# Expert rows: a table of token sums with an adding indirect DMA, in place of a table of expert rows gathered at the end

## Chip, core and metric

The kernel runs on one core of a Trainium2 chip, in float32. The metric is the device time of one execution in microseconds (us), lower is better. The kernel before takes 2435.93 us (median of three runs, 2430.61 to 2442.70).

## What is computed

Two transformer blocks over 512 tokens of width 1024. The change lies in the last part of the second block, the routed experts: 32 experts, each token goes to its four best, and an expert's work is done in blocks of up to 64 rows (slots).

```python
top_vals, top_idx = lax.top_k(logits, TOP_K)              # TOP_K = 4
gates = softmax(top_vals)
# per expert e, on the rows routed to it:
gt = minimum(xb @ w_gate[e] + b_gate[e], 7); up = clip(xb @ w_up[e] + b_up[e], -7, 7)
hid = gt * sigmoid(1.702 * gt) * (up + 1.0)
y_rows = hid @ w_down[e] + b_down[e]
out = zeros.at[row_tok].add(y_rows * row_gate)            # sum of a token's four rows
x = layer_norm(2 ** 0.25 * h + out, ln2_g, ln2_b)
```

## The kernel before

The program is a sequence of stages, each with its own block of instructions per engine and a barrier after it. Everything before the experts (a state-space block, attention, a feed-forward block, the second block's token mixer and router) takes the first 1336 us. The change touches four places: `stage_ffn`, `stage_route`, `stage_experts`, and the shared buffers.

**Routing** (`stage_route`). A one-hot matmul builds, for each slot (column) and partition, the number of the token whose row is worked on there, and its gate. A slot holds 64 rows. Partition p < 64 stands for the first half (512 numbers) of row p, partition 64 + p for its second half, so `G.slot_tokens` holds `2 * token + half`: a row number of the DRAM table `h_halves` (1024 rows of 512). Beside it, `G.choice_row` holds for each token and each of its four choices the row of the table `expert_rows` where the result will lie. A slot's unused rows have gate 0.

**The expert loop** (`stage_experts`). One pass works on one slot. There are 45 passes here for 32 experts (experts with more than 64 rows take more than one). An expert's matrices are three of 4 MB (gate, up, down), loaded by SyncE's queue (SP) as four parts of 1 MB each, two neighbouring matrix rows to a partition, into `expert_ring`: one place for each of the three and a fourth for the next expert's gate matrix, which ScalarE (ACT) copies over (L2405). A part is loaded as soon as the last pass of the expert before has used it (`used`, `moved`), so each pass can also wait for its matrices (`landed`). The order of the experts (`LONG_FIRST`, `PERIOD`) mixes those with more slots among those with one.

TensorE (PE) goes through pass i in this order (L2486): gate product's first half; `turn_up(i-1)` (four transposes); `turn_x(i+1)` (four transposes of the rows of the next slot, which GpSimd has gathered into `slot_x`); gate product's second half; `down(i-1)`; `turn_gate(i)`; up product. Each product has 16 matmul calls (32 instructions). ACT copies products from PSUM; VectorE (DVE) adds biases, clamps, multiplies, and makes in `result(i-1)` (L2555) the tile `slot_y`, the down product times the gates.

GpSimd (POOL) has one task in the loop (L2323): after `turn_x(i)` it copies the row numbers of slot i+1 and issues the indirect DMA (gather) into `slot_x`:

```python
pool.wait_ge(q["x_turned"], i + 1)
gather(i + 1)
```

In pass i+1 ACT stores `slot_y` of slot i with two DMAs (L2394) to `expert_rows`; DVE waits for that (`y_out`) before it writes `slot_y` anew.

**The bias sums.** In the first two passes PE forms `gates @ b_down` for each of the four tiles of 128 tokens (`bias_sum`, L2455), and DVE adds it to `2 ** 0.25 * h` in `G.X` (`add_bias`, L2557).

**The tail.** After the last store has landed, POOL issues 16 indirect gathers from `expert_rows` (`choice`, L2341), three of them adding to what is in SBUF already, because their target is in use; DVE adds thirteen pieces to `G.X` and does the layer norm tile by tile (L2583 to L2602); SP stores the tiles. Rows of `expert_rows` that no pass writes are set to zero in `stage_ffn` (L1279).

Of the kernel before, what the change touches and what calls it, by code (L numbers as in the profile page):

```python
# [1207 lines left out]
def stage_ffn(nc, A, G):  # L1208


    with ExitStack() as ctx:
# [51 lines left out]
        @block.sync  # L1263
        def _(sp):
            ln.load(sp)
            G.W.upto(sp, G.W.index[("q2",)] + RING)
            sp.wait_ge(G.y_zeroed, 16 * (-(-(MAX_SLOTS - EXPERTS) * CAP // P)))
# [6 lines left out]
        def _(act):  # L1274

            act.wait_ge(zeros_ok, 1)
            for r in range(EXPERTS * CAP, MAX_SLOTS * CAP, P):
                n = min(P, MAX_SLOTS * CAP - r)
                act.dma_start(G.y_dram[r:r + n, :], zeros[0:n, :]).then_inc(G.y_zeroed, 16)  # L1279
# [688 lines left out]
def stage_route(nc, A, G):  # L1968
# [6 lines left out]
    with ExitStack() as ctx:  # L1975
# [20 lines left out]
        rowf = sb("choice_rowf", [P, TK])  # L1996
# [84 lines left out]
        def _(dve):  # L2081
# [61 lines left out]
            for h in range(2):  # L2143
# [10 lines left out]
            step(nc.vector.scalar_tensor_tensor(out=rowf[:], in0=sl[:], scalar=float(CAP), in1=col[:], op0=ALU.mult,  # L2154
                                                op1=ALU.add))
            nc.vector.tensor_copy(G.choice_row[:], rowf[:])
# [11 lines left out]
            nc.vector.tensor_scalar(G.slot_tokens[:], ps[:, 3, 0:LIST], upper[:, 0:1], None, ALU.add).then_inc(list_ok, 1)  # L2168

# [51 lines left out]
def stage_experts(nc, A, G):  # L2221
# [5 lines left out]
    with ExitStack() as ctx:  # L2227
# [21 lines left out]
        row_in = [sem(f"ex_row_in{c}") for c in range((T - 1) * TOP_K)]  # L2249
        sum_in, pair_in = sem("ex_sum_in"), sem("ex_pair_in")  # L2250
        pair = X.ring[:, 0, KB - 1, :]

        def plain(n):
            return X.ring[:, X.MATS, n, :] if n < KB else X.ring[:, 0, n - KB, :]
# [26 lines left out]
        def _(sp):  # L2281
# [26 lines left out]
        def _(pool):  # L2308
# [32 lines left out]
            def choice(dst, t, k, sem, add=False):  # L2341
                c = t * TOP_K + k
                at = bass.IndirectOffsetOnAxis(G.choice_row[:, c:c + 1], 0)
                if add:
                    nc.gpsimd.indirect_dma_start(dst, None, G.y_dram[:, :], at, compute_op=ALU.add).then_inc(sem, 16)  # L2345
                else:
                    nc.gpsimd.indirect_dma_start(dst, None, G.y_dram[:, :], at).then_inc(sem, 16)  # L2347
            def four(t):
                for k in range(TOP_K):
                    n = t * TOP_K + k  # L2350
                    choice(plain(n), t, k, row_in[n])
            end = T - 1
            four(0)
            choice(G.X[:, end, :], end, 0, sum_in, True)
            choice(pair, end, 2, pair_in)
            four(1)
            pool.wait_ge(sum_in, 16)
            choice(G.X[:, end, :], end, 1, sum_in, True)
            pool.wait_ge(pair_in, 16)
            choice(pair, end, 3, pair_in, True)  # L2360
            four(2)

        @block.scalar
        def _(act):
# [370 lines left out]
```

## Time and profile before

| | |
|---|---|
| median of three runs | 2435.93 us (2430.61 to 2442.70) |
| profiled execution, its own time | 2436.61 us |
| its span in the trace | 2434.8 us (1.8 us lie around it) |
| first transposes of `slot_x` in the expert stage | at 1336.6 us |
| last matmul ends, DVE starts the last `slot_y` | 2383.3 us |
| end of the span | 2434.8 us |
| busy over the span | PE 2275.0 us (93%), DVE 807.1, ACT 652.7, POOL 206.5 |
| mean granted TensorE clock | 0.959 |
| DMA, whole span | 570.75 MB, 234 GB/s; in the expert loop up to 423 GB/s |

How to read it: times are microseconds from the start of the span. The profile names an instruction by engine, line and operation, `out<-in`. PEclk is the share of the full TensorE clock that was granted (1.00 is 2.4 GHz, 0.50 is 1.2 GHz). "DMA share" is the busy share of the 16 DMA engines. In a timeline the bracket gives the idle time of the engine before the instruction and what ended it. For a DMA issued by POOL, "to landing" runs from the start of POOL's instruction, which first writes the descriptors, to the last byte.

### The profile page before, as it was taken

What the parts mean: (1) busy time and instruction counts of PE and PEld (TensorE: products, weight loads), DVE (VectorE), ACT (ScalarE), POOL (GpSimd) and SP (SyncE); (2) the same over time, 40 slices, a digit from 0 to 9 for tenths busy, and PEclk for the clock granted to TensorE, in tenths of its full rate; (3) what the DMA queues carried; (4) which work ended last, traced back from release to release, by engine and by line L of the source; (5) the groups of instructions that cost most, each with busy time, mean ns of one, the idle gap of its engine ahead of it and who ended that gap; (6) DMA issues with size and microseconds to landing.
All of it is one profiled execution on the core that took longest, in us unless ns stands there. A gap on an engine that the chain in (4) does not pass through costs nothing. (4 is left out here: it accounts for less than half of the span.)

```text
span 2434.8 us, 27490 instructions
## 1 busy us (share of the span) xinstructions
PE 2275.0 (93%) x9835; PEld 1094.8 (45%) x9836; DVE 807.1 (33%) x1548; ACT 652.7 (27%) x854; POOL 206.5 (8%) x239
## 2 busy tenths in 40 slices
PE   6998999989899999989896999999999999999991
PEld 4444656634557567544445333333333333333330
DVE  1411556644444454532434212112111112112125
ACT  1211222221000000001301444444344444444440
POOL 1003111100000000000300000000000000000003
PEclk8999999989999999999896999999999999999995
DMA  8344233210621311141006869999999999999995
GB/s 332 130 191 113 78 87 104 80 68 0 257 102 71 137 69 70 52 157 38 0 27 256 340 240 390 420 423 408 423 422 411 422 408 419 423 406 423 421 381 177
DMA packets 139863, 570.75 MB, mean 234 GB/s; under 512 B 12280, under 2 KB 47277, under 8 KB 88589
## 3 DMA queue, kind: packets, MB, share of 16 engines
q1 hardware_dynamic: 123584, 527.89, 54.8%
q0 software_dynamic: 6432, 21.66, 2.5%
q10 hardware_dynamic: 9772, 20.25, 2.2%
q8 instruction: 42, 0.69, 0.1%
q14 instruction: 33, 0.26, 0.0%
HBM read 545.57 MB, written 24.18 MB: 234 GB/s over the span
## 5 line engine op out<-in xcount | busy, mean ns | idle before, releaser
L2405 ACT COPY expert_ring<-expert_ring 128x2048 f32 x180 | 331.7, 1896 | 70.8 <-DMA expert_ring<-in_w_gate_dram 59.0
L2472 PE MATMUL banks<-expert_ring,slot_xT_gate 128*64 128x512 f32 x1440 | 328.4, 598 | 1.5 <-issue 0.8
L2472 PE MATMUL banks<-expert_ring,hiddenT 128*64 128x512 f32 x1440 | 319.6, 597 | 2.1 <-DVE hiddenT L2547 2.1
L2472 PE MATMUL banks<-expert_ring,slot_xT_up 128*64 128x512 f32 x1440 | 319.6, 595 | 0.8 <-DMA expert_ring<-in_w_up_dram 0.6
L2472 PEld LDWEIGHTS banks<-expert_ring,hiddenT 128*64 128x64 f32 x1440 | 104.0, 138 | 209.5 <-issue 207.2
L2472 PEld LDWEIGHTS banks<-expert_ring,slot_xT_gate 128*64 128x64 f32 x1440 | 100.1, 137 | 188.6 <-issue 181.4
L2472 PEld LDWEIGHTS banks<-expert_ring,slot_xT_up 128*64 128x64 f32 x1440 | 99.1, 137 | 187.1 <-issue 175.9
L2555 DVE TENSOR_SCALAR slot_y<-banks,slot_gates 128x512 f32<-128x512 f32 x45 | 33.8, 750 | 412.4 <-PE banks L2472 412.4
L486 PE MATMUL banks<-hT,weight_ring 128*128 128x512 f32 x320 | 142.6, 605 | 2.3 <-PEq L2642 2.3
L2540 DVE TENSOR_TENSOR up_act_T<-banks,expert_bias_T 128x512 f32<-128x512 f32 x45 | 31.1, 691 | 310.0 <-PE banks L2434 310.0
L1355 PE MATMUL banks<-hT,weight_ring 128*128 128x256 f32 x512 | 114.4, 383 | 4.3 <-PEq L2642 3.3
L1071 PE MATMUL banks<-weight_ring,mix_scaled 128*128 128x512 f32 x256 | 113.6, 605 | 3.5 <-DVE mix_scaled L1109 3.5
L723 PE MATMUL banks<-hT,weight_ring 128*128 128x512 f32 x256 | 115.1, 603 | 0.0
L2379 ACT COPY gate_product<-banks 128x512 f32<-128x512 f32 x45 | 26.4, 586 | 318.3 <-PE banks L2472 318.3
L1355 PEld LDWEIGHTS banks<-hT,weight_ring 128*128 128x128 f32 x512 | 98.1, 192 | 20.5 <-issue 7.0
L486 PEld LDWEIGHTS banks<-hT,weight_ring 128*128 128x128 f32 x320 | 61.4, 194 | 80.8 <-issue 80.8
L1349 PE MATMUL banks<-weight_ring,hidden_T 128*128 128x512 f32 x192 | 84.1, 593 | 0.9 <-PE banks L1355 0.9
L2317 POOL COPY slot_ids<-slot_tokens 128x1 int32 (+1 forms) x45 | 8.2, 183 | 897.6 <-PE banks L2434 897.6
L1355 PE MATMUL banks<-token_half_sums,weight_ring 128*128 128x256 f32 x384 | 84.2, 379 | 0.0
L1071 PEld LDWEIGHTS banks<-weight_ring,mix_scaled 128*128 128x128 f32 x256 | 49.4, 194 | 64.8 <-issue 59.2
L1355 PEld LDWEIGHTS banks<-token_half_sums,weight_ring 128*128 128x128 f32 x384 | 73.0, 190 | 9.9
L723 PEld LDWEIGHTS banks<-hT,weight_ring 128*128 128x128 f32 x256 | 48.1, 193 | 56.2 <-issue 56.2
(440 smaller groups left out, 2500.9 us busy)
## 6 DMA issues: line engine op xcount, KB each, us to landing
expert_ring<-in_w_gate_dram SPq DMA_DIRECT2D x128, 1024.0 KB, 13.5
expert_ring<-in_w_up_dram SPq DMA_DIRECT2D x128, 1024.0 KB, 12.8
expert_ring<-in_w_down_dram SPq DMA_DIRECT2D x128, 1024.0 KB, 10.9
weight_ring<-in_w_ada_dram SPq DMA_DIRECT2D x12, 2048.0 KB, 11.1
weight_ring<-in_w_in_dram SPq DMA_DIRECT2D x8, 2048.0 KB, 14.7
weight_ring<-in_w_ff_in_dram SPq DMA_DIRECT2D x8, 2048.0 KB, 11.1
weight_ring<-in_w_ff_out_dram SPq DMA_DIRECT2D x8, 2048.0 KB, 13.3
weight_ring<-in_w_in_dram SPq DMA_DIRECT2D x24, 512.0 KB, 6.6
```

The lines of the kernel that those rows point to most:

```text
L486: m = nc.tensor.matmul(ps[:, n % 4, :], w[:, k, b * P:(b + 1) * P], G.hT[:, k, :], start=(k == 0), stop=(k == KB - 1))
L723: x = nc.tensor.matmul(out, w[:, k, :], G.hT[:, k, :], start=(k == 0), stop=(k == KB - 1))
L1071: m = nc.tensor.matmul(ps[:, banks[h], :], mix[:, k, t * P:(t + 1) * P], w[:, k % 4, h * HALF:(h + 1) * HALF], start=(k == k0), stop=(k == ...
L1349: m = nc.tensor.matmul(out, x[:, k, j * P:(j + 1) * P], y[:, k, :], start=(k == 0), stop=(k == 3))
L1355: m = nc.tensor.matmul(out[:, b, :], y[:, k, at:at + P], x[:, k, :], start=(k == 0), stop=(k == 3))
L2317: nc.gpsimd.tensor_copy(ids[:], G.slot_tokens[:, at]).then_inc(q["ids_ok"], 1)
L2379: nc.scalar.copy(gate_tok[:], ps[:, B_G, :]).then_inc(q["g_copied"], 1)
L2405: nc.scalar.copy(flat_ring[:, c * size:(c + 1) * size], flat_ring[:, bass.ds(source + c * size, size)])\
L2472: x = nc.tensor.matmul(ps[h * CAP:(h + 1) * CAP, bank, :], lhs[:, k % 4, (k // 4) * CAP:(k // 4 + 1) * CAP], X.ring[:, m, k, h * HALF:(h + ...
L2540: nc.vector.tensor_tensor(up[:], turned_product(B_UT), cols, ALU.add).then_inc(q["u_biased"], 1)
L2555: nc.vector.tensor_scalar(y[:], ps[:, B_D, :], G.slot_gates[:, at], None, ALU.mult).then_inc(q["y_ok"], 1)
```

## The change

Rows are no longer stored to `expert_rows` and gathered at the end. A table `token_sums` in DRAM (2048 rows of 512: 1024 for the tokens' halves, 1024 spare) is first filled with `2 ** 0.25 * h + gates @ b_down`, and each pass adds its `slot_y` to it with one indirect DMA that adds (`add_rows`). At the end the table is read back with four plain loads.

- `stage_ffn`: four DMAs of zeros (the spare rows) in place of sixteen (the unused rows of `expert_rows`).
- `stage_route`: `choice_row` (two instructions) goes; five small DVE instructions after `slot_tokens` form `slot_rows`: for a used row its number `2 * token + half`, for an unused one a spare row.
- POOL: in pass i, `add_rows(i-1)` follows `gather(i+1)`; it waits for `slot_y`, and in pass 1 also for the table (`table_in`). After the loop `add_rows(last)` takes the place of the 16 gathers.
- ACT: `store` goes; in the first two passes four plain DMAs of 512 KB write `G.X` to the table (`to_table`), tile by tile.
- PE and DVE: `bias_sum(2)`, `bias_sum(3)` and their `add_bias` move to an earlier place in pass 1.
- Tail: SP loads the four tiles from the table; DVE has no additions left, only the layer norm.

```diff
 @block.gpsimd
+            def add_rows(i):
+                at = slice(i, i + 1) if isinstance(i, int) else bass.ds(i, 1)
+                pool.wait_ge(q["y_ok"], i + 1)
+                nc.gpsimd.tensor_copy(rows[:], G.slot_rows[:, at]).then_inc(rows_ok, 1)
+                pool.wait_ge(rows_ok, i + 1)
+                if not (isinstance(i, int) and i == 0):
+                    pool.wait_ge(held_rows, i)
+                nc.gpsimd.tensor_tensor(row_tick[:], tick[:, 0:1], tick[:, 0:1], ALU.add).then_inc(held_rows, 1)
+                nc.gpsimd.indirect_dma_start(G.sum_dram[:, :], bass.IndirectOffsetOnAxis(rows[:, 0:1], 0), y[:], None,
+                                             compute_op=ALU.add).then_inc(G.y_out, 16)
             def body(i, first):
                 pool.wait_ge(q["x_turned"], i + 1)
                 gather(i + 1)
+                if first:
+                    pool.wait_ge(table_in, 16 * T)
+                add_rows(i - 1)
...
-            pool.wait_ge(G.y_out, last * 32 + 32)
+            add_rows(last)
+            pool.wait_ge(G.y_out, last * 16 + 16)
             nc.gpsimd.tensor_tensor(tick[:, 2:3], tick[:, 0:1], tick[:, 0:1], ALU.add).then_inc(q["stored"], 1)
-            pool.wait_ge(q["bias_added"], T)
...
 @block.scalar
-            def store(i):
-                act.wait_ge(q["y_ok"], i + 1)
-                for h in range(2):
-                    act.dma_start(G.y_dram[bass.ds(i * CAP, CAP), h * HALF:(h + 1) * HALF],
-                                  y[h * CAP:(h + 1) * CAP, :]).then_inc(G.y_out, 16)
+            def to_table(t):
+                act.wait_ge(q["bias_added"], t + 1)
+                act.dma_start(table(t), G.X[:, t, :]).then_inc(table_in, 16)
...
                 move_gate(i + 1)
-                if not (isinstance(i, int) and i == 0):
-                    store(i - 1)
                 sigmoid(i)
+                if first:
+                    to_table(2 * i)
                 up_copy(i)
+                if first:
+                    to_table(2 * i + 1)
                 x_for_up(i + 1)
 @block.sync
+            sp.wait_ge(q["stored"], 1)
+            for t in range(T):
+                sp.dma_start(G.X[:, t, :], table(t)).then_inc(sums_in[t], 16)
 @block.vector
             def body(i, first):
                 hidden(i - 1)
+                if first:
+                    add_bias(2)
+                    add_bias(3)
                 result(i - 1, first)
                 dve.wait_ge(q["hT_ok"], i)
-                if first:
-                    add_bias(2)
                 gate(i)
-                if first:
-                    add_bias(3)
...
             for t in range(T):
                 x = G.X[:, t, :]
-                for k in range(TOP_K if t < T - 1 else 0):
-                    dve.wait_ge(row_in[t * TOP_K + k], 16)
-                    step(nc.vector.tensor_tensor(x, x, plain(t * TOP_K + k), ALU.add))
-                if t == T - 1:
-                    dve.wait_ge(sum_in, 32)
-                    dve.wait_ge(pair_in, 32)
-                    step(nc.vector.tensor_tensor(x, x, pair, ALU.add))
+                dve.wait_ge(sums_in[t], 16)
                 nc.vector.bn_stats(stats[:, t, 0, :], x[:, 0:HALF])
```

Not shown are the removed function `choice` with its 16 calls (L2341 to L2361) and the small instructions of `stage_route`.

On POOL, the loop of the passes from the second on, before (`slot_ids` are the row numbers of the gather, `tick` is a one-element instruction between):

```order
L2271 UNCONDITIONAL_BRANCH
L2271 ISA
L2317 ISA
L2317 COPY slot_ids<-slot_tokens 128x1
L2318 REGISTER_ALU
L2312 TENSOR_TENSOR tick<-tick 1x1
L2320 DMA slot_x<-h_halves,slot_ids 128x512
L2271 ISA
L2271 COMPARE_AND_BRANCH
```

and with the change (`slot_rows_now` are the row numbers of the adding DMA):

```order
L2276 ISA
L2325 ISA
L2325 COPY slot_ids<-slot_tokens 128x1
L2326 REGISTER_ALU
L2320 TENSOR_TENSOR tick<-tick 1x1
L2328 DMA slot_x<-h_halves,slot_ids 128x512
L2335 ISA
L2335 COPY slot_rows_now<-slot_rows 128x1
L2339 TENSOR_TENSOR row_tick<-tick 1x1
L2340 DMA token_sums<-slot_y,slot_rows_now 2048x512
L2276 ISA
L2276 COMPARE_AND_BRANCH
```

Behind each gather now stands the adding DMA of two slots earlier, and the next pass's gather stands behind that one on the same engine.

On ACT with the change, the end of pass 0, from the sigmoid of pass 0 on:

```order
L2390 ACTIVATE gate_sigmoid_T<-gate_act_T 128x512
L2394 DMA token_sums<-X 128x1024
L2386 COPY up_product<-banks 128x512
L2394 DMA token_sums<-X 128x1024
L2374 COPY slot_xT_up<-banks 128x512
```

The same five rows stand once more at the end of pass 1: the fourth tile's write to the table is issued behind the copy of pass 1's up product.

## Rows read from the trace of the kernel before

**Rows 1.** busy time by stretch: PE, PEld, DVE, ACT, POOL (us), PEclk, DMA share, GB/s

```profile
1400.00:1500.00 100.00, 100.00 (x476) 36.42 (x474) 20.05 (x32) 46.59 (x41) 8.07 (x12) 1.00 0.77 304
1570.00:2300.00 730.00, 728.39 (x3456) 265.78 (x3454) 140.60 (x225) 326.06 (x290) 64.57 (x96) 1.00 1.01 418
```

**Rows 2.** chain that ended last, three stretches of the loop: start us, us, what

```profile
1889.62 20.90 DMA expert_ring<-in_w_up_dram
...
2209.88 20.90 DMA expert_ring<-in_w_up_dram
...
2282.08 1.16 PE banks L2434 x8
...
2293.69 0.68 PE banks L2434 x4
...
2304.82 1.16 PE banks L2434 x8
```

**Rows 3.** who waited for whom, 1500 to 2300, engine PEld: us, times, longest

```profile
PEld banks L2472 <- DMA expert_ring<-in_w_up_dram: 5.5, 8, 1.5
```

**Rows 4.** DMA queues in one pass, 2239.4 to 2262.1: packets, MB, share

```profile
q1 hardware_dynamic: 1239, 9.06, 95.6%
q10 hardware_dynamic: 160, 0.26, 3.0%
```

**Rows 5.** timeline of one pass: start us, us, engine, line, operation [idle <-releaser]

```profile
2283.41 0.18 POOL L2317 COPY slot_ids<-slot_tokens 128x1 int32 x1 [20.48 <-PE banks L2434]
...
2284.26 1.40 POOL L2320 DMA_INDIRECT slot_x<-h_halves,slot_ids  x1 [0.15 <-issue]
...
2286.65 7.04 PE L2472 MATMUL banks<-expert_ring,hiddenT 128*64 128x512 f32 x32
...
2293.93 0.75 DVE L2555 TENSOR_SCALAR slot_y<-banks,slot_gates 128x512 f32<-128x512 f32 x1 [9.14 <-PE banks L2472]
```

**Rows 6.** tile slot_x: the gathers on POOL, and their time to landing

```profile
L2320 POOL DMA_INDIRECT slot_x<-h_halves,slot_ids x45: 987/1397/1400, 1338.5 to 2329.7; - x45
...
DMA to landing us min/median/max: 3.4/7.3/7.7
```

**Rows 7.** timeline, POOL: the second gather, with no DVE work beside it

```profile
1346.80 0.18 POOL L2317 COPY slot_ids<-slot_tokens 128x1 int32<-128x1 int32 x1 [7.26 <-PE banks L2434]
...
1347.55 0.99 POOL L2320 DMA_INDIRECT slot_x<-h_halves,slot_ids  x1 [0.30 <-issue]
```

**Rows 8.** line L2345, the three gathers that add: time on POOL, time to landing

```profile
L2345 POOL DMA_INDIRECT X<-expert_rows,choice_row x2: 1722/1921/2120, 2392.9 to 2403.3; - x2
L2345 POOL DMA_INDIRECT expert_ring<-expert_rows,choice_row x1: 2569/2569/2569, 2405.3 to 2405.3; - x1
...
DMA to landing us min/median/max: 8.4/8.6/9.3
```

**Rows 9.** DMA queue q0, 2402 to 2403.5 (plain), then 2410 to 2411.5 (adding)

```profile
q0 software_dynamic: 165, 0.59, 101.8%
...
q0 software_dynamic: 88, 0.30, 104.3%
```

**Rows 10.** timeline of the last down product and of the tail

```profile
2373.11 9.96 PE L2472 MATMUL banks<-expert_ring,hiddenT 128*64 128x512 f32 x32 [2.09 <-DVE hiddenT L2547]
...
2383.31 0.75 DVE L2555 TENSOR_SCALAR slot_y<-banks,slot_gates 128x512 f32<-128x512 f32 x1 [10.26 <-PE banks L2472]
...
2427.48 0.69 DVE L2592 BATCH_NORM_STATS2 ln2b_stats<-X 128x6 f32<-128x512 f32 x1
...
2430.50 1.28 DVE L2601 SCALAR_TENSOR_TENSOR X<-X,ln2b_mv,hT 128x1024 f32<-128x1024 f32 x1
```

**Rows 11.** tile out_dram, four stores of 512 KB: time to landing

```profile
DMA to landing us min/median/max: 2.6/4.2/6.1
```

**Rows 12.** timeline, pass 1: ACT's copy of the up product

```profile
1386.68 0.59 ACT L2385 COPY up_product<-banks 128x512 f32<-128x512 f32 x1 [4.69 <-PE banks L2472]
```

**Rows 13.** stretch of the last down product (columns as in rows 1)

```profile
2373.10:2379.00 5.90, 5.89 (x14) 1.71 (x16) 0.00 (x0) 0.00 (x0) 0.00 (x0) 0.51 0.02 8
```

More of the change, by code:

```diff
@@ L1266, in _ @@
             G.W.upto(sp, G.W.index[("q2",)] + RING)
-            sp.wait_ge(G.y_zeroed, 16 * (-(-(MAX_SLOTS - EXPERTS) * CAP // P)))
+            sp.wait_ge(G.spare_zeroed, 16 * T)
         @block.gpsimd
@@ L1276, in _ @@
             act.wait_ge(zeros_ok, 1)
-            for r in range(EXPERTS * CAP, MAX_SLOTS * CAP, P):
-                n = min(P, MAX_SLOTS * CAP - r)
-                act.dma_start(G.y_dram[r:r + n, :], zeros[0:n, :]).then_inc(G.y_zeroed, 16)
+            for t in range(T, 2 * T):
+                rows = G.sum_dram[2 * t * P:2 * (t + 1) * P, :].rearrange("(p h) n -> p (h n)", h=2)
+                act.dma_start(rows, zeros[:]).then_inc(G.spare_zeroed, 16)
             for g in range(FG):
@@ L1995, in stage_route @@
         col = sb("choice_col", [P, TK])
-        rowf = sb("choice_rowf", [P, TK])
+        token_row = sb("slot_token_row", [P, LIST])
+        spare = sb("slot_spare", [P, LIST])
+        empty = sb("slot_empty", [P, LIST])
         colhot = sb("col_onehot", [P, TK, P])
@@ L2168, in _ @@
             nc.vector.tensor_scalar(G.slot_tokens[:], ps[:, 3, 0:LIST], upper[:, 0:1], None, ALU.add).then_inc(list_ok, 1)
+            nc.vector.tensor_scalar(token_row[:], ps[:, 3, 0:LIST], upper[:, 0:1], None, ALU.add)
+            step(nc.vector.tensor_scalar(empty[:], ps[:, 3, LIST:2 * LIST], 0.0, None, ALU.is_equal))
+            step(nc.vector.tensor_scalar(spare[:], token_row[:], -1.0, tok[:, 0:1], ALU.mult, ALU.add))
+            step(nc.vector.scalar_tensor_tensor(out=spare[:], in0=spare[:], scalar=2.0 * S, in1=empty[:], op0=ALU.add,
+                                                op1=ALU.mult))
+            nc.vector.tensor_tensor(G.slot_rows[:], token_row[:], spare[:], ALU.add)
 def paired_rows(src, j):
@@ L2248, in stage_experts, with table @@
         held = sem("ex_held")
[L2249 to L2254, printed above, removed]
+        rows, row_tick = sb("slot_rows_now", [P, 1], I32), sb("row_tick", [1, 1])
+        rows_ok, held_rows, table_in = sem("ex_rows_ok"), sem("ex_held_rows"), sem("ex_table_in")
+        sums_in = [sem(f"ex_sums_in{t}") for t in range(T)]
+        def table(t):
+            return G.sum_dram[2 * t * P:2 * (t + 1) * P, :].rearrange("(p h) n -> p (h n)", h=2)
         stats = sb("ln2b_stats", [P, T, 2, 6])
@@ L2334, in _ @@
             pool.wait_ge(G.xg_in, last * 16 + 32)
-            pool.wait_ge(G.y_out, last * 32 + 32)
+            add_rows(last)
+            pool.wait_ge(G.y_out, last * 16 + 16)
             nc.gpsimd.tensor_tensor(tick[:, 2:3], tick[:, 0:1], tick[:, 0:1], ALU.add).then_inc(q["stored"], 1)
             pool.wait_ge(q["stored"], 1)
-            pool.wait_ge(q["bias_added"], T)
[L2341 to L2361, printed above, removed]
         @block.scalar
@@ L2423, in _ @@
             last = loop(act, body)
-            store(last)
             nc.scalar.activation(tick[:, 3:4], tick[:, 0:1], ACT.Sqrt).then_inc(q["root_ok"], 1)
@@ L2496, in body @@
                 turn_x(i + 1)
+                if first and not zero:
+                    bias_sum(2)
                 product(xTg, B_G, 0, range(PARTS // 2, PARTS), now, None if zero else i)
+                if first:
+                    bias_sum(0 if zero else 3)
                 if not zero:
                     down(i - 1, before, not first)
-                if first:
-                    bias_sum(0 if zero else 2)
                 turn_gate(i)
@@ L2506, in body @@
                 product(xTu, B_U, 1, range(PARTS), now)
-                if first:
-                    bias_sum(1 if zero else 3)
+                if zero:
+                    bias_sum(1)
             X.turn_bias(pe, ps, 1).then_inc(q["bias_turned"], 1)
@@ L2564, in body @@
                 hidden(i - 1)
+                if first:
+                    add_bias(2)
+                    add_bias(3)
                 result(i - 1, first)
                 dve.wait_ge(q["hT_ok"], i)
-                if first:
-                    add_bias(2)
                 gate(i)
-                if first:
-                    add_bias(3)
             dve.wait_ge(G.h_out, 16 * T)
```

11 lines of the change are left out of this document (4 added, 7 removed).

## The prediction, made before the changed kernel ran

> **What bounds the kernel now.** I read the busy time by stretch first, then the chain that ended last, then the DMA queues, and last the timeline of one pass. In the loop from 1570 to 2300 us TensorE is busy 728.39 of 730.00 us at the full clock, and the 16 DMA engines have a share of 1.01 at 418 GB/s; only from 1400 to 1500 do they have room (0.77) [rows 1]. So two resources are full at once. The chain shows a pass as TensorE's own work: from 2282.08 to 2304.82 us, that is 22.74 us [rows 2]. It also shows that every seven passes a part of an up matrix lands just when it is needed: such waits begin at 1889.62 and at 2209.88 us, 320.26 us apart for 14 passes, or 22.88 us a pass [rows 2], and the weight loads waited eight times for up parts, 5.5 us in all [rows 3]. Nothing is left over on the DMA engines there: in one pass the expert matrices take a share of 95.6% and the stores of `slot_y` 3.0% [rows 4].
>
> About 0.5% (12 us) is what a measurement of this kernel can tell from no change. The sum below is made against the profiled execution's own 2436.6 us, 0.7 us above the median of the runs.
>
> **The tail: 20 us less.** Before, from the start of the last `slot_y` at 2383.31 us [rows 10] to the end of the span are 51.5 us. With the change: `slot_y` is done at 2384.06. POOL wakes 0.17 us after its releaser (the transposes end at 2283.24 [rows 2], the copy starts at 2283.41), and needs 0.85 us from that copy to its DMA instruction [rows 5]: 2385.1. The adding DMA on a quiet core: the fastest gather lands 3.4 us after its start [rows 6]; I add 0.8 us for descriptors and 0.7 us for the transfer (both below), so it lands at about 2390.0. The tick on POOL and SP's issue take 0.4 us, a load of 512 KB 4.2 us (the stores of that size have this median [rows 11]), so DVE starts at 2394.6. A tile of the layer norm takes 4.3 us (2427.48 to 2430.50 + 1.28 [rows 10]), four take 17.2: 2411.8. The last store took 3.0 us to the end of the span: 2414.8, which is **20.0 us** earlier. Bounds: 15 (the adding DMA lands after 9.3 us [rows 8]) and 22 (the load lands after 2.6 us [rows 11]).
>
> **The first table: 16.5 us more.** `add_rows(0)` in pass 1 waits for all four writes of `G.X` to the table, and the fourth is issued by ACT behind `up_copy(1)`, so after pass 1's up product. Behind that wait stands, on POOL, the gather for slot 3, which TensorE needs at `turn_x(3)` in pass 2. Count from the end of the up product: the copy is done after 0.64 us (0.59 and a wake of 0.05 [rows 12]), the write is issued at 0.75, lands after 6 us (my choice between 4.2 and something above 6.1 [rows 11], since weights are loading) at 6.75. Then POOL: 0.17 + 0.85 + 2.0 (descriptors of the adding DMA) + 0.3 + 0.75 + 6.9 (gather, both from the next part) = 10.97, so the rows are there at 17.7. TensorE is there 3.9 us after the up product (11.61 less 0.68 less 7.04, below). It stands still for 13.8 us. After an idle stretch of 2.09 us before the last down product the granted clock was 0.51 [rows 13], the lower level of 1.2 GHz, and the product took 9.96 us [rows 10] in place of 7.04 [rows 5]: 2.9 us more. Together 16.7, say **16.5 us**. Bounds: 7 (table in 4.2 us, descriptors 1.0, gather 3.4, no fall of the clock) and 21.
>
> **The loop: 30 us more.** Two things are added to each pass, and both end in TensorE's waits.
>
> First the order on POOL. Until now the gather for slot i+2 started right behind `turn_x(i+1)`. Now it stands behind `add_rows(i-1)`, which waits for `slot_y` of `down(i-1)` in the same pass. Count from the end of that product, at 2293.69 us [rows 2]. `slot_y` is done at 2294.68, so at 0.99 [rows 5]. POOL wakes (0.17) and reaches its DMA instruction (0.85) at 2.01. Writing descriptors takes a plain gather 1.40 us in the loop [rows 6] and 0.99 without DVE work beside it [rows 7], an adding one 1.72 to 2.57 us in the tail [rows 8]: I take 2.0, since DVE works beside only part of it, and get 4.0. Then 0.3 us between two such instructions, 0.75 us from copy to DMA instruction with DVE quiet [rows 7]: 5.06. A gather lands 7.3 us after its start [rows 6], less the 0.4 us by which its descriptors are now faster: 11.96. TensorE needs the rows at `turn_x`: the eight transposes of the next pass end at 2305.98 and the last four take 0.68 [rows 2], so at 2305.30, or 11.61. It waits **0.4 us** a pass. The unshown price is that of the adding DMA in front: low end 1.0 us of descriptors, the rows are 0.6 us early; high end 2.57 us and a gather that lands as late as the slowest adding one, 9.3 us [rows 8], a wait of 3.4 us. I take the inner value because adding DMA and gather are issued 3 us apart, more than the DMA engines need for either.
>
> Second the DMA engines. An adding DMA keeps them longer for the same bytes: 165 plain packets of 0.59 MB in 1.5 us against 88 adding ones of 0.30 MB [rows 9], so 2.6 against 5.2 us for a MB. The store took 3.0% of a pass, 0.68 us [rows 4]; the adding DMA of the same 0.26 MB takes 1.36, **0.7 us** more a pass. Where the engines are full, from 1570 us to the end of the loads at some 2370, that is 35 passes: 24 us. Before that there is room.
>
> The two waits overlap: an idle stretch for one lets the other catch up. I count the 24 us, and 6 us for the passes before 1570 us and for passes in which the gather is the later one. Low end nothing, if loads and gathers find room; high end 3.4 us in each of 42 passes, 143 us, and then the clock: if it falls behind each of them as it did behind the idle 2.09 us, 2.9 us more a pass, 122 us.
>
> **At nothing.** TensorE's work is the same; bias sums only change places, each `add_bias` (1.2 us) has a half gate product of 3.6 us beside it. ACT loses two DMA issues a pass and waits for TensorE anyway. The zeros in `stage_ffn` are written beside matmuls that show no gap; five short DVE instructions in `stage_route` run while POOL prepares the first gather. If that cover were gone they cost about 1 us.
>
> **Sum:** 2436.6 - 20 + 16.5 + 30 = **2463 us**.
>
> **A page against the row.** The gather's 7.3 us carry the loop's first term [rows 6]. The Trainium skill, "DMA: Bandwidth & Descriptors", section "Anatomy of one DMA", fits a DMA issued from GpSimd as 2.0 us plus its bytes at 436 GB/s, which is an estimate of 2.6 us for these 256 KB. The trace does not agree: the row is 4.7 us above the page's figure, with the DMA engines at a share of 1.01, and the row decides.
>
> **The rivals.**
> - **Gathers land as on a quiet core** (3.4 us, least of [rows 6], in place of 7.3). Then they are never late in the loop, only the 24 us of the DMA engines remain, and the start is 3.5 us shorter: 2436.6 - 20 + 13 + 24 = 2454 us. Against it: the median is near the maximum of 7.7. The page's fit named above would have it come out this way.
> - **The loop becomes a chain through POOL.** It decides where the gather's wait is well above the 0.7 us a pass of the DMA engines; if the clock falls behind the waits too, slower products lie on the same chain. With 1.85 us (2.57 us of descriptors, 0.85 and 7.7 us for the gather) it is 2436.6 - 20 + 16.5 + 78 = 2511 us, with 3.4 us and the clock up to 2698. For it: descriptors in the tail took up to 2.57 us. Against it: less loading while TensorE waits should make gathers faster.
> - **The loop takes it for nothing.** The additional 0.7 us fit in and gathers come in time; the start costs its 16.5 us or somewhat less: about 2436 us, no difference. For it: SP waits for free buffers in most passes.
> - **Faster, by the tail.** As the last, and the wait for the first table costs only its lower bound of 7 us: 2436.6 - 22 + 7 = 2422 us. It decides at a start and a loop that cost less than 8 us together. For it: from 1400 to 1500 us the DMA engines had room. Against it: the fourth write lies behind an up product, whatever the transfer takes.
>
> **How the numbers follow.** My forecast has a chance of 0.45 (2450 to 2490 us), the chain through POOL 0.20, quiet gathers 0.07, nothing in the loop 0.15, faster by the tail 0.13. Slower by over 0.5% are the first three: 0.72. Within 0.5%: 0.15. Faster: 0.13. The range of 2430 to 2550 leaves out the last rival and the upper part of the chain through POOL, 2 in 10 together.
>
> **What would show it.** TensorE waiting at L2434 for `slot_x` in most passes, or for up parts longer than before, with passes of 23.2 to 23.7 us between the same transposes; one wait of 10 to 17 us near 1393 us, with PEclk at 0.50 behind it; the adding DMA at twice the store's share; 31 us from the last `slot_y` to the end. I am wrong if passes stay at 22.8 us (then the loads had room), if they exceed 25 us (then the chain through POOL rules), or if the wait near 1393 us is missing.

## The result, and the profile after

The changed kernel takes **2559.12 us** (median of 4 runs, 2557.15 to 2563.89) against 2435.55 us: the ratio is 1.0514, 95% interval 1.0494 to 1.0534, so it is 5% slower. The forecast was 2463 us with a range of 2430 to 2550. The span of the profiled execution is 2562.2 us, 127 us more than before.

The stretches of [rows 1], in the trace after. Columns: stretch, us, then PE, PEld, DVE, ACT, POOL busy, PEclk, DMA share, GB/s.

```profile
1400.00:1500.00 100.00, 92.34 (x418) 33.17 (x420) 15.68 (x25) 40.13 (x36) 14.49 (x24) 0.94 0.64 233
1570.00:2300.00 730.00, 673.18 (x3022) 240.84 (x3020) 122.17 (x196) 282.15 (x252) 101.49 (x168) 0.96 0.94 365
```

Neither of the two resources that were full is full any more: TensorE is busy 673 of 730 us, the DMA engines have a share of 0.94, and the granted clock is below 1. Something else sets the pace. The waits of TensorE name it (engine, line, waited for; us, times, longest), from 1300 us on:

```profile
PE banks L2434 <- DMA slot_x<-h_halves,slot_ids: 98.8, 43, 12.5
```

and the gathers themselves, in the tile view of `slot_x`, which answers to [rows 6]:

```profile
L2328 POOL DMA_INDIRECT slot_x<-h_halves,slot_ids x45: 987/1028/1049, 1336.7 to 2488.9; - x45
...
DMA to landing us min/median/max: 3.5/9.3/10.0
```

No wait for an up matrix [rows 3] is left. TensorE waits for the gather in 41 of the 42 passes behind the 12.5 us at the start (the last of the 43 waits lies at the start too), and the gather's median landing went from 7.3 to 9.3 us although its descriptors are written faster (1.03 in place of 1.40 us). One pass on POOL and on TensorE, in the timeline (start, us, engine, line, operation, idle before and its releaser), answers to [rows 5]:

```profile
1796.04 7.04 PE L2472 MATMUL banks<-expert_ring,hiddenT 128*64 128x512 f32 x32
...
1804.25 0.18 POOL L2335 COPY slot_rows_now<-slot_rows 128x1 int32 x1 [20.30 <-DVE slot_y L2557]
...
1805.04 1.84 POOL L2340 DMA_INDIRECT token_sums<-slot_y,slot_rows_now  x1 [0.34 <-issue]
...
1807.50 1.03 POOL L2328 DMA_INDIRECT slot_x<-h_halves,slot_ids  x1 [0.15 <-issue]
...
1816.86 0.90 PE L2434 MATMUL banks<-ident,slot_x 128*128 128x128 f32 x4 [1.98 <-DMA slot_x<-h_halves,slot_ids]
1817.69 5.13 PE L2472 MATMUL banks<-expert_ring,slot_xT_gate 128*64 128x512 f32 x16
```

The down product ends at 1803.08, the gather starts 4.42 us later and lands 9.3 us after that; TensorE stands idle 1.98 us. Then the second half of the gate product takes 5.13 us; before, it took 3.65 us in every one of these passes. The stretch of that half (columns as above) has a granted clock of 0.69, a mixture of the two levels of 2.4 and 1.2 GHz:

```profile
1817.70:1822.60 4.90, 4.90 (x17) 1.56 (x18) 0.00 (x0) 0.00 (x0) 0.00 (x0) 0.69 1.01 428
```

The page's group for the whole gate products puts a sum on that, before and after:

```profile
L2472 PE MATMUL banks<-expert_ring,slot_xT_gate 128*64 128x512 f32 x1440 | 328.4, 598 | 1.5 <-issue 0.8
```

```profile
L2472 PE MATMUL banks<-expert_ring,slot_xT_gate 128*64 128x512 f32 x1440 | 373.2, 666 | 0.7 <-ACT slot_xT_gate L2371 0.7
```

The same 1440 matmuls take 44.8 us more. Counted over the timeline, 27 of the 42 second gate halves of the loop were slow (4.8 to 5.4 us each), the other 15 took 3.65 us. The waits ahead of the slow ones were 1.72 to 2.62 us long, those ahead of the others up to 2.31, so the length of the wait alone doesn't decide it. The passes are of two lengths, 24.5 to 25.4 and 26.2 to 27.3 us, mean 26.08 against 22.81.

The start and the tail, again from the timeline:

```profile
1394.33 0.18 POOL L2335 COPY slot_rows_now<-slot_rows 128x1 int32<-128x1 int32 x1 [47.90 <-DMA token_sums<-X]
...
1403.15 1.12 PE L2434 MATMUL banks<-ident,slot_x 128*128 128x128 f32 x4 [12.47 <-DMA slot_x<-h_halves,slot_ids]
1404.21 5.36 PE L2472 MATMUL banks<-expert_ring,slot_xT_gate 128*64 128x512 f32 x16
...
2531.51 0.75 DVE L2557 TENSOR_SCALAR slot_y<-banks,slot_gates 128x512 f32<-128x512 f32 x1 [9.08 <-PE banks L2472]
...
2533.20 1.59 POOL L2340 DMA_INDIRECT token_sums<-slot_y,slot_rows_now  x1 [0.33 <-issue]
2538.25 0.18 POOL L2361 TENSOR_TENSOR tick<-tick 1x1 f32<-1x1 f32 x1 [3.46 <-DMA token_sums<-slot_y,slot_rows_now]
```

**Where the time is:** the tail is 30.7 us long (2531.51 to 2562.2) in place of 51.5, so -20.8. The waits for `slot_x` are 98.8 us: 12.5 at the start, 84.1 in the 41 waits of the loop (2.05 each), and 2.2 for one of the first gathers, which was waited for before as well (2.5), so +96.3. The gate products are +44.8, the transposes of `slot_x`, slower behind a wait, +6.4 (36.5 in place of 30.1). Together +126.7 of the +127.4 us; terms of under 4 us, which go both ways, are left out.

### The profile page after: what moved, and what is told of

It reads as the page before. It is cut to its first block and busy times, and to the rows that moved or that the text cites. A ratio compares the mean times of both kernels' runs of the same rounds, so it can differ in the third digit from the quotient of the medians.

```text
span 2562.2 us, 27405 instructions
## 1 busy us (share of the span) xinstructions
PE 2329.9 (91%) x9835; PEld 1107.3 (43%) x9836; DVE 793.3 (31%) x1538; ACT 652.3 (25%) x854; POOL 258.1 (10%) x358
## 5 line engine op out<-in xcount | busy, mean ns | idle before, releaser
L2472 PE MATMUL banks<-expert_ring,slot_xT_gate 128*64 128x512 f32 x1440 | 373.2, 666 | 0.7 <-ACT slot_xT_gate L2371 0.7
L2472 PEld LDWEIGHTS banks<-expert_ring,slot_xT_gate 128*64 128x64 f32 x1440 | 110.2, 152 | 223.6 <-issue 217.2
L2434 PE MATMUL banks<-ident,slot_x 128*128 128x128 f32 x184 | 36.5, 325 | 98.8 <-DMA slot_x<-h_halves,slot_ids 98.8
L2335 POOL COPY slot_rows_now<-slot_rows 128x1 int32 (+1 forms) x45 | 8.2, 182 | 999.4 <-DVE slot_y L2557 951.5
L1355 PEld LDWEIGHTS banks<-hT,weight_ring 128*128 128x128 f32 x512 | 98.1, 192 | 20.5 <-issue 7.0
L486 PEld LDWEIGHTS banks<-hT,weight_ring 128*128 128x128 f32 x320 | 61.0, 193 | 80.1 <-issue 80.1
L1349 PE MATMUL banks<-weight_ring,hidden_T 128*128 128x512 f32 x192 | 84.1, 593 | 0.9 <-PE banks L1355 0.9
L2340 POOL DMA_INDIRECT token_sums<-slot_y,slot_rows_now x45 | 82.5, 1833 | 15.3 <-issue 15.3
```

Of the source, the lines that this page charges most:

```text
L486: m = nc.tensor.matmul(ps[:, n % 4, :], w[:, k, b * P:(b + 1) * P], G.hT[:, k, :], start=(k == 0), stop=(k == KB - 1))
L1349: m = nc.tensor.matmul(out, x[:, k, j * P:(j + 1) * P], y[:, k, :], start=(k == 0), stop=(k == 3))
L1355: m = nc.tensor.matmul(out[:, b, :], y[:, k, at:at + P], x[:, k, :], start=(k == 0), stop=(k == 3))
L2340: nc.gpsimd.indirect_dma_start(G.sum_dram[:, :], bass.IndirectOffsetOnAxis(rows[:, 0:1], 0), y[:], None, compute_op=ALU.add).then_inc(G.y_ ...
L2434: m = nc.tensor.transpose(ps[:, bank, j * P:(j + 1) * P], paired_rows(src, j), G.ident[:])
L2472: x = nc.tensor.matmul(ps[h * CAP:(h + 1) * CAP, bank, :], lhs[:, k % 4, (k // 4) * CAP:(k // 4 + 1) * CAP], X.ring[:, m, k, h * HALF:(h + ...
```

## The experiments

The expectations name the experiments by label: e1 add later, e2 plain scatter, e3 gather first, e4 the fourth write to the table earlier, e5 and e9 plain scatter with a pause, e6 later and plain, e7 and e8 `move_gate` split, e10 adding with a pause, e11 another order of loads. The ratios are against the kernel before on the same chip: 2433.39 us for e1 to e4 (19 runs), 2433.58 for e5 to e8 (9), 2434.24 for e9 to e11 (15). A difference under 0.5% is taken as none.

### The order on POOL

**Add later.** POOL adds the rows of slot i-2 behind gather(i+1), so that no wait for `slot_y` of the same pass stands ahead of a gather. The diff leaves out two lines on the counting of `row_tick`.

```diff
             def body(i, first):
                 pool.wait_ge(q["x_turned"], i + 1)
                 gather(i + 1)
-                if first:
+                if not first:
                     pool.wait_ge(table_in, 16 * T)
-                add_rows(i - 1)
+                    add_rows(i - 2)
...
+            add_rows(last - 1)
             add_rows(last)
```

> Edit: pass i adds slot i-2's rows (ready half a pass after the gather of slot i+1 was issued) in place of slot i-1's, so GpSimd is free again when the next gather is due. Theory A (order on POOL: the gather starts 4.4 us after the down product and queues behind the adding DMA): TensorE waits for slot_x in no pass, the wait near 1390 us goes too, granted clock 1.00 through the loop. Theory B (the doubled engine time of the adding DMA slows the loads and all that hangs on them): waits for up parts stay or grow, the time stays above 2500. By A alone 2435.5 - 21 = 2415 us; with the predicted 24 us of DMA engine time on top, 2439 us.

Measured: 2429.23 us, ratio 0.9983 (0.9973 to 0.9993): no difference from before. The 124 us are gone with one step of POOL's order, with every add intact, so theory B falls; the time lies between the two values given for A. In its trace the gathers land at 7.3 us again, with the same adding DMAs on the same queue, each now issued 11.4 us ahead of the next gather in place of 2.5. What is left shows in the waits of TensorE from 1570 to 2300 us:

```profile
PE banks L2435 <- ACT up_product L2387: 12.1, 5, 3.8
```

**Gather first.** The other way round: POOL still waits for `slot_y`, but then issues gather(i+2) ahead of the adding DMA (gather(2) goes ahead of the loop; the diff leaves out that line and a longer `slot_tokens`).

```diff
             def body(i, first):
-                pool.wait_ge(q["x_turned"], i + 1)
-                gather(i + 1)
                 if first:
                     pool.wait_ge(table_in, 16 * T)
+                pool.wait_ge(q["y_ok"], i)
+                pool.wait_ge(q["x_turned"], i + 2)
+                gather(i + 2)
                 add_rows(i - 1)
```

> Edit: POOL still waits for slot_y of slot i-1, but then issues the gather (of slot i+2) first and the adding DMA behind it. This takes away only the DMA in front of the gather. Theory A with the queueing as the larger part: the gather starts 1.9 us after the down product and lands after about 7.0 us, at 8.9 of the 11.6 us that there are, so no waits in the loop; a wait of some 9 us for the first table remains. 2435.5 - 21 + 12 = 2427 us, with 24 us of DMA engine time 2451 us. If the wait comes from the engines' load and not from the queue, the gather still takes over 9 us, and there are waits of about 0 to 1 us: 2440 to 2480 us.

Measured: 2446.16 us, ratio 1.0055 (1.0038 to 1.0072). From its tile view of `slot_x`:

```profile
DMA to landing us min/median/max: 3.3/7.2/8.4
```

Both experiments bring back 7.2 to 7.3 us. The time of gather first lies between the 2427 and the 2451 us of its expectation, nearer to the one with the adds' engine time. The two differ in the first wait: 11.0 us stay here, since POOL still waits for the table there.

**Plain scatter.** The order of the changed kernel, with `compute_op` taken off, so that the same bytes are written and not added (the sums are left out).

> Edit: the changed kernel with its per-pass DMA writing without adding (the sums are left out, so the layer norm works on other numbers). Theory A: the gather still starts 4.4 us after the down product, so it still waits; behind a DMA of half the engine time it should land some 0.7 us sooner than 9.3, so waits of about 1.3 us a pass in place of 2.1, fewer falls of the clock, 2490 to 2530 us. Theory B: with the adding gone the loop returns to 22.8 us a pass: about 2430 us.

Measured: 2429.54 us, ratio 0.9980 (0.9970 to 0.9991). The number is the one of theory B: the waits of 1.3 us a pass that A expected are missing. The gather starts 4.17 us after the down product and 2.21 us after the scatter, much as in the changed kernel, but in the loop it is in time (three waits of up to 0.3 us). Timeline of POOL, then the tile view of `slot_x`:

```profile
1810.70 1.24 POOL L2340 DMA_INDIRECT token_sums<-slot_y,slot_rows_now  x1 [0.33 <-issue]
...
1812.91 1.00 POOL L2328 DMA_INDIRECT slot_x<-h_halves,slot_ids  x1 [0.15 <-issue]
```

```profile
DMA to landing us min/median/max: 3.4/7.3/7.9
```

So the 2 us of landing are not the order alone and not the add alone: they need an adding transfer directly in front. The landings of the transfers in front show how the 2 us come about (medians in the loop). The plain scatter lands 7.3 us after its start and the gather 2.1 us behind it; in the changed kernel the adding DMA lands 9.8 us after its start and the gather 2.0 us behind it. Both transfers are still under way when the gather starts, but the adding one lands 2.5 us later, and the gather with it.

**Adding with a pause.** Is the gather's landing tied to its own start, or to the transfer in front? The changed kernel, adds intact, with an addition on POOL between the two that is there for its time alone:

```diff
+        pause_cols = sb("pause_cols", [P, 500])
...
                 pool.wait_ge(q["x_turned"], i + 1)
+                pool.wait_ge(paused, i)
+                nc.gpsimd.tensor_tensor(pause_cols[:], pause_cols[:], pause_cols[:], ALU.add).then_inc(paused, 1)
                 gather(i + 1)
```

> The changed kernel (adds intact) with one POOL instruction over 128x500 floats, about 1.0 us, between the adding DMA and the gather. The gather starts 1.0 to 1.5 us later than in the changed kernel (5.4 to 5.9 us after the down product's end in place of 4.4). Theory 'the gather's packets stand behind the adding ones in the same queue, so that its landing is set by when those are through': slot_x lands at the same time as in the changed kernel, 8 to 8.3 us after the start in place of 9.3, and the time stays within 2552 to 2570. Rival 'each gather takes 9.3 us whenever it starts while an adding one runs': 1.0 to 1.5 us more per pass, 2595 to 2620.

Measured: 2563.55 us, ratio 1.0530 (1.0514 to 1.0546); the changed kernel has 1.0514. The gather starts 5.87 us after the down product (4.42 in the changed kernel), and in the pass shown TensorE begins on the rows 13.74 us after it (13.78). Timeline, then tile view:

```profile
1810.14 1.03 POOL L2330 DMA_INDIRECT slot_x<-h_halves,slot_ids  x1 [0.16 <-issue]
```

```profile
DMA to landing us min/median/max: 3.4/8.0/8.6
```

A start 1.45 us later costs nothing (passes of 26.11 in place of 26.08 us), and the gather again lands 2.0 us behind the adding transfer: that one sets the landing. The rival would have cost 1.0 to 1.5 us a pass.

### Lateness without an adding transfer

The plain scatter again (sums left out), with the pause between scatter and gather, once of 900 and once of 1500 columns.

> The kernel of e2_plain_scatter (the scatter doesn't add, so the sums are left out) with one more POOL instruction in each pass, an addition over 128x900 floats between the scatter and the gather's id copy, some 2.0 us by the 128x512 that took 1.04 and the 128x1024 that took 2.35. The gather then starts about 6.4 us after the down product's end, lands 7.3 us later, and is 2 us late in each pass, with no adding transfer anywhere. Theory 'the lateness is the whole loss, by itself and by the clock that falls after it': 2545 to 2560 us, waits of about 2 us for slot_x in all passes of the loop and gate halves of 5.1 to 5.4 us behind more than half of them. Rival 'the adding transfers are what costs, in engine time and in lateness both': the time stays within 2430 to 2500.

> The kernel of e5_plain_pause (scatter without adding, so the sums are left out) with the POOL instruction between scatter and gather widened from 128x900 to 128x1500 floats: 1.70 us there, so 2.8 us here. In e5 the gather started 6.0 us after the down product's end, slot_x came 1.1 to 1.2 us late in each pass, the clock stayed at 1.00 and the time was 2487. Here it starts about 7.1 us after and is late by 2.2 to 2.4 us, as in the changed kernel. Theory 'a wait of 2 us before the second gate half lets the clock fall, one of 1.1 us doesn't': gate halves of 5.1 to 5.4 us come back behind more than half of the waits, granted clock of the loop 0.95 to 0.97, 2545 to 2565 us. Rival 'the clock falls in the changed kernel for another reason, the adding transfers among them': only the longer wait, 1.1 us times 43 more, 2530 to 2538, and the clock stays at 1.00.

Measured: 2487.47 us, ratio 1.0230 (1.0206 to 1.0254), for the shorter; **2582.91 us**, ratio 1.0602 (1.0586 to 1.0618), for the longer. For each, the waits of TensorE and the stretch from 1570 to 2300; first 900 columns:

```profile
PE banks L2438 <- DMA slot_x<-h_halves,slot_ids: 60.1, 43, 11.5
```

```profile
1570.00:2300.00 730.00, 696.47 (x3258) 253.61 (x3258) 175.92 (x213) 303.16 (x270) 150.66 (x210) 1.00 0.97 394
```

then 1500 columns, with the page's group of the gate products as well:

```profile
PE banks L2438 <- DMA slot_x<-h_halves,slot_ids: 110.6, 43, 11.9
```

```profile
1570.00:2300.00 730.00, 666.95 (x2962) 237.62 (x2960) 187.40 (x193) 280.00 (x248) 167.63 (x193) 0.95 0.89 356
```

```profile
L2476 PE MATMUL banks<-expert_ring,slot_xT_gate 128*64 128x512 f32 x1440 | 385.5, 685 | 0.7 <-ACT slot_xT_gate L2375 0.7
```

The first expectation was set for a lateness of 2 us and got 1.17 (47.8 us in the 41 waits of the loop), since the gather started 5.9 and not 6.4 us after the down product and landed after 7.0: the time lies in the rival's range, but by a shorter lateness than either theory spoke of, so this run decided nothing, and the second was made for that. It shows what the lateness costs nearly alone: 3 of 42 gate halves were slow, and passes have a mean of 24.31 us, 1.5 over before. The second has 2.36 us (96.7 in 41 waits), 34 of 42 gate halves slow, 57 us more of gate products than before, passes of 26.67 us. It is slower than the changed kernel and contains no adding transfer. The pause also made VectorE's work longer (187 us busy in place of 122), but from 1570 to 2300 us TensorE waited for `slot_x` alone. So a late gather alone costs that much, by the wait and the clock behind it; and since TensorE waits for no matrix in the changed kernel, nothing there points to another cost of the adding DMA than that it makes the gather late. The time is 18 us above the range expected: 34 slow halves are more than the "more than half" that it was worked out with.

### The DMA engines

**Later and plain.** The first experiment without `compute_op` (sums left out).

> The kernel of e1_add_later with compute_op taken from the scatter (the sums are left out): what is left between e1's 2429 us and this is the adding itself. Theory 'the adding transfer's second 0.7 us of engine time per pass makes the gate matrices late, and that is what e1 lost': the passes of 23.6 to 26.9 us shrink to under 23.5, the wait of the up product's turns for its copy (12.8 us, 6 times in e1) goes, and the time is 2412 to 2420. Rival 'any indirect transfer of 256 KB there delays them': passes and time as in e1, 2426 to 2432.

Measured: 2411.38 us, ratio 0.9907 (0.9892 to 0.9923); against "add later" the adding costs 0.76%, or 18 us. That is the first theory's time, less 1 us, and TensorE's waits for the up copy are 2.4 us in place of 12.8. DMA queues, 1600 to 2290 us (packets, MB, share of 16 engines), adding and then plain:

```profile
q0 software_dynamic: 6576, 15.47, 8.8%
```

```profile
q0 software_dynamic: 4880, 15.99, 5.8%
```

3.0% of 690 us over some 30 passes are 0.69 us a pass, beside the 0.7 of the forecast. The mean pass goes from 23.19 to 22.85 us (14 us over 42 passes), and 2 us are in the tail. The long passes come every seventh pass, and the timeline of ACT and TensorE in the kernel that adds later shows how a late matrix reaches TensorE there:

```profile
1888.42 1.90 ACT L2405 COPY expert_ring<-expert_ring 128x2048 f32 x1 [9.06 <-DMA expert_ring<-in_w_gate_dram]
...
1899.37 0.57 ACT L2387 COPY up_product<-banks 128x512 f32<-128x512 f32 x1
...
1899.99 1.13 PE L2435 MATMUL banks<-ident,up_product 128*128 128x128 f32 x4 [3.76 <-ACT up_product L2387]
```

A gate matrix lands late, ACT waits 9.06 us for it with `up_copy` behind it in its own order, and TensorE waits 3.76 us for that copy.

**Two attempts to go round it.** Splitting `move_gate` on ACT, two parts ahead of the up copy and two behind, in "add later" and, alone, in the kernel before (there with one more wait on POOL after the loop, not shown):

```diff
                 x_for_gate(i + 1)
-                move_gate(i + 1)
+                move_gate(i + 1, range(PARTS // 2))
                 sigmoid(i)
...
                 up_copy(i)
...
                 x_for_up(i + 1)
+                move_gate(i + 1, range(PARTS // 2, PARTS))
```

> The kernel of e1_add_later (adds intact), and on ACT the copies of the next gate matrix are issued in halves: two parts before the sigmoid and the up product's copy, two behind them. In e1 the up product's copy stood behind four gate copies that waited up to 9.1 us for their matrix, and PE's turn of the up product waited for that copy 12.8 us in 6 waits, with the gate half behind it at the low clock. Theory 'the order on ACT turns the late gate matrix into a wait of PE': those waits go, 2410 to 2418 us. Rival 'the matrix itself is late': the wait moves to the second gate half, on the ring copies, and the time stays 2426 to 2432.

> The kernel before with the same reordering of the gate copies on ACT alone. It waits 3.2 us for the up copy in all (weight loads, four times), so by the theory of e7 it gains 2 to 5 us: 2428 to 2432. Rival 'the order on ACT is worth 15 us anywhere': 2420 or less. If the second gate half waits for its copies in steady passes: 2440 and more.

Measured: 2483.07 us (ratio 1.0203, 1.0189 to 1.0217) and 2499.77 us (1.0261, 1.0245 to 1.0277). In the first run both theories fall, in the second the two on the order on ACT; of its third case ("2440 and more") only the number came, since the waits for the copies are 4.1 us in all and those for up matrices 26.2. The waits for the up copy go, but TensorE now waits for matrices (first kernel, 1570 to 2300 us):

```profile
PE banks L2474 <- DMA expert_ring<-in_w_up_dram: 21.2, 37, 1.6
PE banks L2474 <- ACT expert_ring L2405: 14.2, 15, 1.5
PE banks L2474 <- DMA expert_ring<-in_w_down_dram: 6.5, 10, 0.9
```

with a DMA share of 0.97 there, where "add later" has 1.02. What fits: the later copies give the gate buffer back later, SP issues all loads in one order behind that wait, and the DMA engines run dry. SP's waits that an ACT copy ended did grow in that stretch, from 198.3 to 257.2 us; that they are the cause was not tried.

The other attempt moves a gate load on SP ahead of an up load, in "add later": `GATE_TURN = (0, 0, 2, 0, 2)` for `(0, 1, 2, 0, 2)`.

> The kernel of e1_add_later (adds intact) with SP's table of load orders changed at one place, GATE_TURN = (0, 0, 2, 0, 2) in place of (0, 1, 2, 0, 2): the gate matrix that landed late every seventh pass (9.1 us of wait on ACT, up to 3.8 us on PE behind it) is issued ahead of the up matrix and not behind it. Theory 'the DMA engines are full, so that whichever matrix gives way comes late': the wait moves to the up matrix, 2428 to 2440. Rival 'only the order is wrong': the long passes go, 2411 to 2420, which would be 1% under the kernel before.

Measured: 2431.92 us, ratio 0.9990 (0.9981 to 0.9999). The time is that of "add later" or slightly more, and the wait moved to the up matrix, as the first theory has it:

```profile
PE banks L2473 <- DMA expert_ring<-in_w_up_dram: 15.7, 17, 1.6
```

### The first table

The fourth write to the table is issued by ACT ahead of the up copy of pass 1, not behind it:

```diff
+                if first and not (isinstance(i, int) and i == 0):
+                    to_table(3)
                 up_copy(i)
-                if first:
-                    to_table(2 * i + 1)
+                if first and isinstance(i, int) and i == 0:
+                    to_table(1)
```

> Edit: the fourth write to the table is issued by ACT before its copy of pass 1's up product. Both theories: the write starts at about 1381.3 in place of 1386.6 us and lands at about 1390 in place of 1394.2, so the one wait of 12.5 us near 1390 becomes about 8 us; the loop stays as it is: 4 us less than the changed kernel, 2555 us.

Measured: 2553.62 us (2 runs), ratio 1.0494 (1.0473 to 1.0515), an interval that overlaps the changed kernel's. The time is near the 2555 us expected, but the wait of 8 us is not there; the first wait is nearly what it was:

```profile
1390.27 1.65 POOL L2340 DMA_INDIRECT token_sums<-slot_y,slot_rows_now  x1 [0.17 <-issue]
...
1399.93 1.12 PE L2436 MATMUL banks<-ident,slot_x 128*128 128x128 f32 x4 [12.17 <-DMA slot_x<-h_halves,slot_ids]
```

All of TensorE's work came 3 us earlier in this execution (the turn of the up product at 1387.01 in place of 1389.94), and the adding DMA 4.7 us earlier, so against TensorE it began some 1.7 us sooner: the fourth write, issued right behind the third, took 11.0 us to land in place of 7.6. And the gather behind the adding DMA took 7.4 us from its start to TensorE's turn (1392.54 to 1399.93), where it took 5.9 in the changed kernel (1397.21 to 1403.15), and that gave 1.5 us back. Whether the loads that were under way by then are the reason was not tried.

## Why the prediction was wrong

**The tail** held: -20.8 us against -20.0. Each piece came within 0.7 us of its cost; the quiet adding DMA took 5.05 us from its start to POOL's tick (2533.20 to 2538.25), for which the sum had 4.9.

**The first table** held in its size, in part because errors cancelled: a wait of 12.5 us against 13.8, at 1403 us with the slow gate half behind it. The fourth write landed after 7.6 us, not 6; POOL needed 1.0 us less from there to the gather, and the gather 1.0 us less to land. What the clock cost was 1.7 us (5.36 - 3.65) and not 2.9, since only half a product ran slowly. Together 14.2 us against 16.5. The experiment that adds later takes the wait for the table and the one for `slot_y` from in front of this gather, and its pass there takes 26.70 us in place of 39.34 (26.71 before). Gather first, which keeps the wait for the table, keeps 11.0 of the 12.5 us.

**The loop** is where it failed: +137 us (42 passes of 3.27 us) against +30. The right rival was "the loop becomes a chain through POOL", which had a chance of 0.20; its low case of 2511 us was still 48 us short, since it had no slower clock in it. By the forecast's own sign (passes over 25 us) that rival is the one. The step that failed is the term for the order on POOL, which put the wait at 0.4 us, with the words "I take the inner value because adding DMA and gather are issued 3 us apart, more than the DMA engines need for either". Term by term:

- **The start of the gather** was right, even cautious: 5.06 us forecast, 4.42 measured (the adding DMA took 1.84 us on POOL, and the gather's id copy overlapped it).
- **The landing** was mis-sized: 6.9 us forecast, 9.3 measured. The argument was about how long DMA engines work on one transfer (1.36 us), not about how long the transfer is under way: the adding one lands 9.8 us after its start in the loop, and the gather 2.0 us behind it. With a plain scatter in front, which lands after 7.3 us, the same gather lands at 7.3; with a pause ahead of it its landing stays where it was in the pass. The high end had the same 9.3 us, taken from the slowest adding gather of the tail [rows 8]; that is another kind of transfer in another place, so the agreement is chance. 4.42 + 9.3 less the 11.61 of the forecast is 2.1 us, and 2.05 was measured.
- **The clock** was left at the high end only. The forecast had seen it fall behind an idle stretch of 2.09 us [rows 10, 13] and costed it at 2.9 us for the last down product. At waits of 2.05 us in mean it fell behind 27 of 41, 43 us by the slow halves, 1.6 us each: only half a product ran slowly, not a whole one as in the 2.9. At 1.17 us it fell behind 3 of 41, at 2.36 behind 34. A wait's price here is not proportional to its length.
- **The DMA engines.** The engine time was sized right (0.69 us a pass), but in the changed kernel it shows in no wait for a matrix: while TensorE waits for gathers, the engines have a share of 0.94. Only where the gather is in time does it appear: 18 us for the whole kernel, 14 of them in the loop, where the forecast had 24. And it enters mostly not at an up matrix as forecast, but at a gate matrix, by way of ACT's order. "The two waits overlap" was therefore right in kind, and the wrong one of the two was counted.
- **The argument against the rival** ("less loading while TensorE waits should make gathers faster") fell: with a plain scatter and a DMA share of 0.89 gathers took 7.2 us (the pause of 1500 columns), at 1.01 they took 7.3.

The rival of gathers that land as on a quiet core found no support: in no run whose trace shows the landings did the gathers of the loop have a median under 7.0 us. The fit in the Trainium skill, "DMA: Bandwidth & Descriptors", section "Anatomy of one DMA", from which the estimate of 2.6 us for these bytes came, doesn't agree with these rows.

The Trainium skill, "DMA: Bandwidth & Descriptors", section "Two DMAs through the same engine are not ordered", says that within one queue of a DMA engine descriptors start in order and are pipelined. The paused experiment agrees as far as it goes: a gather issued 1.45 us later landed at the same place in the pass. Why an adding transfer lands 2.5 us later than a plain one, where its engine time is 0.7 us more, no run shows.

## What to carry to other kernels

A DMA that has to be in time doesn't go behind another on the same queue just because the engines' time would allow it: add up starts and landings along the queue, and take the landing from a row that had such a transfer in front. Here moving the adds one pass back, behind the gather, turned 5% slower into no difference (0.9983, 0.9973 to 0.9993): the tail's 21 us are nearly used up by what the adding costs (18 us). Where a stall of TensorE is near the length at which a row of the same kernel shows the clock falling, price the slower products too, before choosing the inner value of a range.

## What was not expected of the hardware

- An adding indirect DMA of 256 KB directly in front on POOL's queue made the next gather land after 9.3 us; a plain one of the same bytes left it at 7.3. In both cases the gather landed 2.0 to 2.1 us behind the one in front, which took 9.8 us when it added and 7.3 when it didn't.
- In the loop adding descriptors cost POOL 1.84 us against 1.24 for plain ones (1.59 against 0.99 in the tail).
- Behind 41 idle stretches of TensorE of 1.17, 2.05 and 2.36 us in mean, 3, 27 and 34 gate halves were slow, with the same work before and behind them. A slow one took up to 5.4 us in place of 3.65; in the one measured the granted clock was 0.69.
- Copying half of a buffer later on ACT cost 54 us (2483 against 2429), though ACT was busy for only 304 of the 730 us from 1570 to 2300.
